# Splitting each block of weights into high and low parts with one cast and one subtraction instead of two of each

## What is computed

```python
h = jnp.einsum('bsd,de->bse', x, w_in[l])            # first block: all branches' inputs
merged = merged + gates[:, :, i] * jnp.einsum('bsc,cd->bsd', branches[i], w_branch[l, i])
out = jnp.einsum('bsd,de->bse', merged, w_out[l])
...
proj = h @ w_in                                      # second block
x = x + jnp.concatenate([y_ssd, y_fox], axis=-1) @ w_out
x = x + peer(rmsnorm(x, ln2_w), peer_wq, peer_k1, peer_k2, peer_u, peer_v)
```

## Time and profile before

| | |
|---|---|
| median of 3 runs | 3694.01 us |
| span of the profiled execution | 3698.0 us (4.0 us above the median; the sum below is made against this span) |
| PE matmuls busy | 3393.0 us, 92% |
| DVE busy | 2099.8 us, 57% |
| ACT busy | 1482.7 us, 40% |
| mean granted TensorE clock | 0.962 of full speed |
| from the HBM | 603 MB moved in all, mean 163 GB/s |

### The profile page before, as it was taken

One profiled execution on the slowest core, in us unless ns is written; L12 is line 12 of the kernel. 1 busy time (PEld: TensorE's weight loads), 2 busy tenths in 40 slices (PEclk: granted clock), 3 DMA queues, 4 the chain that ended last, 5 costly groups with the idle time before them and its releaser, 6 DMA issues.

```text
span 3698.0 us, 66856 instructions
## 1 busy us (share of the span) xinstructions
PE 3393.0 (92%) x27030; PEld 3343.6 (90%) x27030; DVE 2099.8 (57%) x3116; ACT 1482.7 (40%) x1934; POOL 28.8 (1%) x43
## 2 busy tenths in 40 slices
PE   7888878999999989998879958799999999999998
PEld 7878768999999979998779947799999999999998
DVE  4446885645545456673353998665555555555554
ACT  4444324444444334343234423343434343434343
POOL 0000000000000000000000000000000000000000
PEclk9989999999999999999889979999999999999999
DMA  8323333455555534433134424555555554545553
GB/s 273 128 92 125 138 140 121 170 184 183 184 182 182 184 124 148 148 127 113 58 120 176 159 93 158 205 204 182 204 181 204 181 204 181 204 181 204 182 182 114
DMA packets 84439, 603.35 MB, mean 163 GB/s; under 512 B 8976, under 2 KB 9136, under 8 KB 15328
## 3 DMA queue, kind: packets, MB, share of 16 engines
q1 hardware_dynamic: 76752, 557.88, 41.9%
q0 software_dynamic: 7328, 43.52, 3.6%
q10 hardware_dynamic: 240, 0.26, 0.0%
HBM read 579.60 MB, written 22.02 MB: 163 GB/s over the span
## 4 chain that ended last, share of the span: by engine, by line
PE 79%; DVE 15%; ACT 2%; issue 2%; DMA 1%; DVEq 1%; ACTq 0%; SPq 0%
PE bank L348 24%; PE bank L350 24%; PE bank L349 24%; DVE wlo L333 4%; DVE dacc L989 3%; ACT whi L327 2%; PE bank L484 1%; DVE one L1396 1%; PE bank L481 1%; DMA raw<-stream 1%; PE bank L408 1%; DVE one L1390 1%; PE bank L495 1%; PE bank L907 0%; DVEq L989 0%
## 5 line engine op out<-in xcount | busy, mean ns | idle before, releaser
L333 DVE TENSOR_TENSOR wlo<-raw,whi 128x1024 fp32r<-128x1024 f32 x1056 | 1286.6, 1225 | 1262.0 <-ACT whi L327 1244.6
L327 ACT CAST whi<-raw 128x1024 fp32r<-128x1024 f32 x1056 | 1101.9, 1046 | 1538.3 <-PE bank L350 1518.6
L348 PE MATMUL bank<-xhi,whi 128*128 128x256 f32 x5360 | 1535.4, 286 | 87.4 <-DVE wlo L333 63.0
L349 PE MATMUL bank<-xlo,whi 128*128 128x256 f32 x5360 | 1524.2, 284 | 0.0
L350 PE MATMUL bank<-xhi,wlo 128*128 128x256 f32 x5360 | 1523.7, 284 | 0.0
L348 PEld LDWEIGHTS bank<-xhi,whi 128*128 128x128 f32 x5360 | 1036.3, 193 | 97.4 <-DVE wlo L333 55.4
L349 PEld LDWEIGHTS bank<-xlo,whi 128*128 128x128 f32 x5360 | 1036.1, 193 | 0.7
L350 PEld LDWEIGHTS bank<-xhi,wlo 128*128 128x128 f32 x5360 | 1035.4, 193 | 0.0
L348 PE MATMUL bank<-aghi,whi 128*128 128x256 f32 x2048 | 583.4, 285 | 12.9 <-DVE aglo L1417 12.0
L349 PE MATMUL bank<-aglo,whi 128*128 128x256 f32 x2048 | 580.2, 283 | 0.0
L350 PE MATMUL bank<-aghi,wlo 128*128 128x256 f32 x2048 | 580.1, 283 | 0.0
(11 more groups left out here) (338 smaller groups left out, 2461.3 us busy)
## 6 DMA issues: line engine op xcount, KB each, us to landing
raw<-stream SPq DMA_DIRECT2D x528, 1024.0 KB, 4.8
gate_matrix<-gstage POOLq DMA_DIRECT2D x8, 2048.0 KB, 7.6
gslice<-gate_matrix POOLq DMA_DIRECT2D x8, 2048.0 KB, 9.3
relative_band<-cband POOLq DMA_DIRECT2D x1, 3072.0 KB, 37.2
xraw<-xt SPq DMA_DIRECT2D x1, 2048.0 KB, 7.9
cbias<-relative_band POOLq DMA_DIRECT2D x1, 2048.0 KB, 20.8
xagain<-xt POOLq DMA_DIRECT2D x1, 2048.0 KB, 8.7
out<-zsum SPq DMA_DIRECT2D x4, 512.0 KB, 2.6
```

Source lines behind the costliest of these rows:

```text
L327: nc.scalar.copy(whi[b.half][:, k, :], raw[b.raw][:, k, :]).then_inc(hi_done, 1)
L333: nc.vector.tensor_tensor(wlo[b.half][:, k, :], raw[b.raw][:, k, :], whi[b.half][:, k, :].bitcast(f32), ALU.subtract).then_inc(lo_done, 1)
L348: nc.tensor.matmul(o, whi[b.half][:, k, :], rhi[:, r, :], start=i == 0, stop=False)
L349: nc.tensor.matmul(o, whi[b.half][:, k, :], rlo[:, r, :], start=False, stop=False)
```

## The change

`split_hi` and `split_lo` do a whole block at once. The cast has 2048 columns and waits for `mm_done` of block b; the wait for `mm_half` is gone. The subtraction has 2048 columns and waits for that cast. Both add 2 to their semaphores at their end, so PE's two waits in a block are met together. Where the upward blocks of a slice ask for the halves apart, the whole block is split where the first half stood.

```diff
         def split_hi(act, b, halves=(0, 1)):
-            for h in halves:
-                k = slice(8 * h, 8 * h + 8)
-                if h == 0:
-                    act.wait_ge(raw_loaded[b.raw], 16 * b.uses())
-                if b.n0 >= SPLIT:
-
-                    act.wait_ge(mm_done if h else mm_half, b.count(1 - SPLIT))
-                nc.scalar.copy(whi[b.half][:, k, :], raw[b.raw][:, k, :]).then_inc(hi_done, 1)
+            if 0 not in halves:
+                return
+            act.wait_ge(raw_loaded[b.raw], 16 * b.uses())
+            if b.n0 >= SPLIT:
+
+                act.wait_ge(mm_done, b.count(1 - SPLIT))
+            nc.scalar.copy(whi[b.half][:, :, :], raw[b.raw][:, :, :]).then_inc(hi_done, 2)
 
         def split_lo(dve, b, halves=(0, 1)):
-            for h in halves:
-                k = slice(8 * h, 8 * h + 8)
-                dve.wait_ge(hi_done, 2 * b.count() + h + 1)
-                nc.vector.tensor_tensor(wlo[b.half][:, k, :], raw[b.raw][:, k, :],
-                                        whi[b.half][:, k, :].bitcast(f32), ALU.subtract).then_inc(lo_done, 1)
+            if 0 not in halves:
+                return
+            dve.wait_ge(hi_done, 2 * b.count() + 2)
+            nc.vector.tensor_tensor(wlo[b.half][:, :, :], raw[b.raw][:, :, :],
+                                    whi[b.half][:, :, :].bitcast(f32), ALU.subtract).then_inc(lo_done, 2)
```

## The result

The kernel with the change takes 3829.05 us (median of four runs, 3826.08 to 3831.03), the one before 3693.99 us (3693.6 to 3695.03). The ratio is 1.0365, with a 95% interval of 1.035 to 1.0379: 3.65% slower, 135 us. The forecast was 3807 us with a range of 3778 to 3832.

The account below looks back on a forecast made before the run. It took PE as the bound in some stages, and elsewhere the time from a block's last matmul until DVE is free. Terms summed to 113.5 us on 3698.0, less 4.0 for the profiled execution: 3807 us, range 3778 to 3832.

Parts of the forecast that it names:

- The likeliest case: The forecast itself for the whole kernel: 3807 us, 3.1% slower, spanning 3790 to 3825; chance 0.72.
- 1. A chain behind the split: Where DVE work that PE waits for stands behind the split: 1.92 us later at 36 places, +69.1 us.
- 2. Halves that no longer overlap: Halves back to back at 7 places, +5.7 us; PE waiting for the split at 4, +4.3: together +10.0 us.
- Merge, the step that failed: In merge, block b+1 hides the later split with 1.2 us to spare: no idle time of PE.
- 3. and 4. Evacuations, state-space heads: Evacuations behind the longer cast, 4 places, +3.4 us; state-space heads, 0.94 for each of 7 pairs, +6.6 us.
- 5. From upward to downward blocks: In 6 slices, PE gets aglo at the first downward block's middle 2.82 us later: +16.9 us.
- 6. Less per instruction: One subtraction is shorter than two where DVE is the bound, 32 convolution and 18 routing blocks: -3.5 us.
- 7. Clock: New stops at the 6 slices and the start of merge lower PE's clock, 1.6 us more each: +11 us.
- (a): The slices' upward blocks become bound by ACT and DVE; turns of 6.0 us would add 23 us: 3830; chance 0.08.
- (b): PE's longer waits in attentions and slices cost more clock: 3827; if no new stop lowers it, 3796; chance 0.10.
- (c): Half of the DVE chains behind the split are covered, giving 35 us instead of 69: 3773; chance 0.07.
- (d): In all stages the block in between hides the split; only the cost per instruction shows: 3690; chance 0.03.

Follow-up runs that it names:

- e3: Casts and subtractions in halves as in the kernel before, but both casts wait for mm_done, in the whole split's place: 3772.22 us, ratio 1.0205.
- e8: Opposite of the change: the split in three parts of 8, 4 and 4 chunks, the last waiting for mm_done: 3656.01 us, ratio 0.9893 to the kernel before.
- e1: The kernel with the change, but its subtraction in two halves again, both behind the one whole cast: 3813.91 us, ratio 1.0319.
- e7: The kernel with the change, with Copy in place of Sigmoid on merge's gates, so that ACT's table loads there fall away: 3816.61 us, ratio 1.033.
- e4: The kernel before, halves and waits kept, with only the change's order in the upward blocks of the slices: 3702.44 us, ratio 1.0016.
- e5: The kernel before, with the whole split and its order in the six slices alone: 3716.2 us, ratio 1.0056.

## Why the prediction was right, point by point

The forecast's sum was 113.5 us against 126.3 in the spans. The medians differ by more (135) because the span profiled of before is 4.0 us above its median and that with the change 4.7 us below. The likeliest case came true, with the sum 13 us short. That it is not further off is in part luck: the clock at the slices and the state-space heads were priced some 8 us too high, and merge and the chain 13 us too low. Its terms by stage (by rounding they add up to 113.9):

| stage | forecast | measured |
|---|---|---|
| first attention and convolution | 16.7 | 15.7 |
| norms, branches a and b | 8.2 | 11.6 |
| start of merge, with its clock | 3.5 | 4.5 |
| merge | 0 | 7.5 |
| w_out, norms, dt | 5.8 | 10.2 |
| state-space branch | 11.3 | 11.6 |
| second attention | 15.4 | 17.9 |
| w_out2, routing | 2.6 | 4.4 |
| one-hot matrices | 15.4 | 15.6 |
| early slices | 1.9 | 3.3 |
| six slices, with their clock | 26.5 | 22.9 |
| up to the first attention | 0 | 1.4 |
| evacuations and waits for a first half, not placed | 6.6 | in the stages above |

**1. A chain behind the split: right, and a little small.** Not 1.92 but 2.07: the subtraction starts 2.00 us after the cast began and not 1.93, and the one cast starts 0.12 us after PE's last matmul ended (163.66 - 5.32 = 158.34, cast at 158.46), where the second half's cast started 0.04 after it. Each one-hot part grew by 2.07 and PE's wait for cprob by as much. In 36 places that would be 5.4 us. e3 and e8 show the same chain at two other lengths.

**2. Halves that no longer overlap: right, too few.** PE waits for the split itself at more places than my four: e1, which gives PE its first half back and nothing else, is 15 us faster than the change, and not by the clock alone (the slices' 2.8). The norms and the stages from w_out to dt cost 3.4 and 4.4 us more than forecast; e1 gives back 3.1 and 1.6 of it, and where the rest stands is open.

**Merge, the step that failed.** I priced merge at nothing, with a cover of 1.2 us. That holds in eleven of twelve blocks. At the turn of the loop it doesn't; timeline of ACT with the change, and in the lower two rows DVE and PE:

```profile
802.51 0.41 ACT L1570 CAST mhi<-msum 128x256 f32 x1 [4.16 <-DVE msum L1102]
803.06 1.28 ACT L326 ACT_TABLE_LOAD   x1
804.35 1.90 ACT L326 CAST whi<-raw 128x2048 fp32r<-128x2048 f32 x1
...
806.36 2.29 DVE L332 TENSOR_TENSOR wlo<-raw,whi 128x2048 fp32r<-128x2048 f32 x1 [2.85 <-ACT whi L326]
...
808.70 0.38 PE L347 MATMUL bank<-xhi,whi 128*128 128x256 f32 x1 [0.83 <-DVE wlo L332]
```

The cast before it began at 796.45 and PE's blocks take 5.76, so this one was due at 802.21. It starts 2.14 late: ACT first makes mhi, whose msum stands on DVE behind the whole split, and then loads its table for 1.28. The split ends at 808.65 and PE stops for 0.83. Before, the same load was there (ACT, 767.74), but the halves ended early enough. This comes once in 12 blocks and costs 1.1 each time, seven times in the stage. e7 takes the load away and the growth with it; e1, with the load, gives PE its first half 1.1 earlier and has no growth either. So neither the load nor the later first half stops PE by itself, and the late msum alone doesn't either (e7 has it still): it takes them together. The row of ACT_TABLE_LOAD was in the trace of before; I had averaged over the stage and not looked at the turn of the loop. The Trainium skill (ScalarE: Activation LUTs, What ACT_TABLE_LOAD costs) gives 1283 ns for a load, which the row confirms, and 1380 ns of drain with it, which it doesn't: from the end of mhi's cast to the start of the next there are 1.43 us in all.

**3. and 4. Evacuations, state-space heads.** The evacuations' 3.4 us can't be told apart in the stages; no run shows them. The heads grew by 0.6 us a pair, not 0.94 (the rows that I read, 1571.38 and 1572.41, leave 1.03 of slack, so the term should have been 0.89); the stage as a whole came out right by luck, because its entry cost more.

**5. From upward to downward blocks: right in mechanism and size.** Timeline with the change, ACT, DVE, PE at the place of the earlier trace rows:

```profile
2764.66 1.90 ACT L326 CAST whi<-raw 128x2048 fp32r<-128x2048 f32 x1 [0.42 <-PE bank L349]
...
2768.87 0.58 DVE L1435 TENSOR_TENSOR gated<-gelu,gslice 128x256 f32<-128x256 f32 x1
2770.14 0.43 DVE L1441 TENSOR_TENSOR aglo<-gated,aghi 128x256 f32 x1 [0.68 <-ACT aghi L1695]
...
2770.62 0.38 PE L347 MATMUL bank<-aghi,whi 128*128 128x256 f32 x1 [3.17 <-DVE aglo L1441]
```

PE is on at T + 5.96; forecast T + 5.80, before T + 2.98. Six times 2.98 is 17.9, forecast 16.9. e4 shows the part of it that the order alone makes, about a third, and e5 that the loss is there without the other stages'.

**6. Less per instruction: too many places.** In the convolution each block should have been 0.07 us shorter; from its start to its end the growth rises by 0.4 us instead of falling by 2.2. DVE is busy there for 162.32 of 200.00 us and so not the bound throughout. In the routing the 0.07 us is seen where DVE never stops: the blocks there (2131 to 2157 in the trace of before, the place of the earlier trace rows) are 0.06 to 0.08 us shorter with the change. But they are four, not eighteen; the routing as a whole grew.

**7. Clock: half right.** At the start of merge the clock fell as forecast: after a stop of 4.70 us (737.01) it is 0.56 over the next 3.2 us, and matmuls start 0.21 us apart instead of 0.12. For each of the six slices I took 1.6 us. Windows from PE's restart in each, with the change:

```profile
2770.60:2775.30 4.70, 4.68 (x26) 4.68 (x27) 0.00 (x0) 0.00 (x0) 0.00 (x0) 0.64 0.97 411
2959.90:2964.40 4.50, 4.50 (x27) 4.50 (x28) 0.00 (x0) 0.00 (x1) 0.00 (x0) 0.67 0.98 411
3148.50:3152.10 3.60, 3.19 (x26) 3.19 (x27) 0.35 (x1) 0.00 (x0) 0.07 (x1) 1.00 0.89 350
3336.20:3339.80 3.60, 3.14 (x26) 3.14 (x27) 0.40 (x1) 0.00 (x0) 0.12 (x1) 1.00 0.92 348
3524.00:3527.60 3.60, 3.20 (x26) 3.20 (x27) 0.34 (x1) 0.00 (x0) 0.06 (x1) 1.00 0.98 360
3712.10:3716.60 4.50, 4.36 (x26) 4.39 (x27) 0.00 (x0) 0.00 (x1) 0.00 (x0) 0.69 0.53 215
```

After the same stop of 3.2 us PE ran much of the half block at 1.2 GHz in three slices and none of it in the other three. The boundaries grew by 4.8, 4.6, 3.3, 3.3, 3.3 and 4.5 us, so the three cost 1.2 to 1.5 us each, 4.0 of the 9.6 forecast. The Trainium skill (TensorE: Matmul & The Clock Gate, What's actually happening) has two clocks only, which agrees with the 0.12 and 0.21 us above, and says that the count of slow matmuls varies from run to run; here it varies within a run.

**The rivals.** (a), a bound ring in the upward blocks: from the first slice on the six stops for aglo are PE's only idle stretches over 0.2 us, and the period of the upward blocks stays 5.76. (b), the clock: in the second attention the seven pairs have 14.6 us more idle time of PE (7 x 2.07) and 2.0 us more busy time for the same matmuls (from 98.48 to 100.44 us, the granted clock from 0.87 to 0.83), which is the clock's part; in the first attention it gave something back. The sign that I had named for (b), a clock below 0.88 in the attentions, came in both (0.86 and 0.84), so it doesn't tell what the clock costs: PE's busy time for the same work does. (c), half of the chains covered: the one-hot parts and PE's waits say no. (d), not slower: excluded; what speaks for it, less work for DVE and ACT, is in the profile and worth nothing.

## What to carry to other kernels

Where two engines hand a block on to each other, its pieces should be judged by what still has to be done after the release: there one large instruction costs the lost overlap and the lost head start, and a smaller last piece (here a quarter of a block, 1.1% of the whole time) wins although every instruction has its fixed cost (two subtractions of 1024 columns take 2.45 us, one of 2048 takes 2.29). Check the cover of a "hidden" edit at the turn of each loop and not in the stage's mean, since a table load or a late sum may have used it up already. And read how many rows one matmul of the program makes in the trace before its time is used as a price, and what a wait added for an experiment is itself released by.

## What the hardware showed that I had not expected

The cost of the low clock doesn't grow with the wait that brings it: 2.0 us a pair after a wait of 2.29, 3.3 after 4.44, 2.3 after 5.32, and before, with the waits all 3.25, two values in turn (2.3 and 3.4). Stops of the same 3.2 us lowered the clock after three of six with the change, after one of six in e1 and two of six in e5, whose stops are as long; the shorter stops of e3 (2.26 us) lowered it after four of six, and those of e4 (1.15 us) after none. Two windows behind the stops, the second slice of e3 and the second of e1:

```profile
2908.60:2911.80 3.20, 3.19 (x15) 3.19 (x16) 0.00 (x0) 0.00 (x0) 0.00 (x0) 0.50 0.94 394
2951.10:2954.30 3.20, 3.20 (x26) 3.20 (x27) 0.00 (x0) 0.00 (x0) 0.00 (x0) 1.00 0.93 389
```

So a part of any gain or loss by a shorter or longer wait of PE, up to 1.5 us each time, is luck of this kind, and can be in either direction.
